# Reordering around the first down columns and the first products of a seven-product feed-forward layer

## What is computed

```python
def swiglu(x, w_gate, w_up, w_down):
    return (jax.nn.silu(x @ w_gate) * (x @ w_up)) @ w_down

h = h + 0.5 * swiglu(rms_norm(h, ffn1_norm[l]), ffn1_w_gate[l], ffn1_w_up[l], ffn1_w_down[l])
...
h = h + 0.5 * swiglu(rms_norm(h, ffn2_norm[l]), ffn2_w_gate[l], ffn2_w_up[l], ffn2_w_down[l])
```

## Time and profile before

| | us |
|---|---|
| median of 3 runs (1808.31 to 1810.58) | 1808.53 |
| the profiled execution | 1809.8 |
| its span, first to last instruction | 1808.0 |
| PE busy (98%) | 1776.7 |
| DVE busy (68%) | 1221.9 |
| ACT busy (47%) | 850.2 |
| POOL busy (15%) | 265.7 |

### The profile page before, as it was taken

The page is one execution under the profiler, slowest core; times in us unless marked ns, Lnnn a source line. Parts: engine busy times, 40 slices in busy tenths (PEclk is TensorE's granted clock), DMA queues, the critical chain, the costliest instruction groups (busy, mean ns, idle before and its releaser), DMA issues.

```text
span 1808.0 us, 24821 instructions
## 1 busy us (share of the span) xinstructions
PE 1776.7 (98%) x9474; PEld 1510.5 (84%) x9474; DVE 1221.9 (68%) x1473; ACT 850.2 (47%) x1197; POOL 265.7 (15%) x270
## 2 busy tenths in 40 slices
PE   9989999999999999989999999999999999999997
PEld 7779989888777788869989988888888888888886
DVE  6577737543677665577746658877577586869884
ACT  5345425433555544335524446454353454466673
POOL 3001101121000002001101140110201102213332
PEclk9999999999999999999999999999999999999999
DMA  6235434244321234324534223232222222233333
GB/s 237 94 102 154 140 113 121 82 144 121 109 86 56 65 102 146 121 94 136 156 107 144 77 87 108 88 100 94 83 92 88 93 88 76 93 98 101 105 128 105
DMA packets 56151, 195.94 MB, mean 108 GB/s; under 512 B 6680, under 2 KB 8856, under 8 KB 56048
## 3 DMA queue, kind: packets, MB, share of 16 engines
q1 hardware_dynamic: 39408, 135.55, 22.9%
q0 software_dynamic: 16208, 58.55, 10.8%
q10 hardware_dynamic: 432, 0.40, 0.1%
HBM read 190.26 MB, written 2.11 MB: 106 GB/s over the span
## 4 chain that ended last, share of the span: by engine, by line
PE 88%; DVE 4%; issue 4%; DMA 2%; ACT 1%; POOL 0%; ACTq 0%; DVEq 0%; POOLq 0%
PE banks L635 23%; PE banks L637 22%; PE banks L636 22%; PE banks L752 4%; PE banks L753 3%; PE banks L754 3%; DMA m<-matrices 2%; DVE w_lo L2054 1%; PE banks L845 1%; PE banks L864 1%; PE banks L888 1%; PE banks L1025 1%; PE banks L1023 1%; PE banks L1024 1%; ACT w_hi L1433 1%
## 5 line engine op out<-in xcount | busy, mean ns | idle before, releaser
L2050 DVE TENSOR_TENSOR w_lo<-w_raw,w_hi 128x1024 fp32r<-128x1024 f32 x249 | 317.1, 1274 | 324.3 <-ACT w_hi L1321 323.2
L1321 ACT ACTIVATE w_hi<-w_raw 128x1024 fp32r<-128x1024 f32 x249 | 263.2, 1057 | 359.3 <-PE banks L637 320.3
L635 PE MATMUL banks<-u_hi,w_hi 128*128 128x512 f32 x1016 | 400.6, 394 | 0.9 <-DVE u_lo L2067 0.9
L637 PE MATMUL banks<-u_hi,w_lo 128*128 128x512 f32 x1016 | 395.8, 390 | 0.0
L636 PE MATMUL banks<-u_lo,w_hi 128*128 128x512 f32 x1016 | 395.4, 389 | 0.0
L635 PEld LDWEIGHTS banks<-u_hi,w_hi 128*128 128x128 f32 x1016 | 190.8, 188 | 42.6 <-issue 2.5
L637 PEld LDWEIGHTS banks<-u_hi,w_lo 128*128 128x128 f32 x1016 | 190.7, 188 | 40.6
L636 PEld LDWEIGHTS banks<-u_lo,w_hi 128*128 128x128 f32 x1016 | 190.9, 188 | 38.7 <-issue 0.5
L2054 DVE TENSOR_TENSOR w_lo<-m,w_hi 128x1024 fp32r<-128x1024 f32 x96 | 116.8, 1222 | 67.4 <-ACT w_hi L1433 67.4
L752 PE MATMUL banks<-xs_hi,w_hi 128*128 128x256 f32 x512 | 147.8, 289 | 12.4 <-DVE w_lo L2054 10.1
L1433 ACT ACTIVATE w_hi<-m 128x1024 fp32r<-128x1024 f32 x96 | 100.2, 1052 | 101.8 <-DMA m<-matrices 46.7
(11 more groups left out here) (383 smaller groups left out, 3384.8 us busy)
## 6 DMA issues: line engine op xcount, KB each, us to landing
w_raw<-weights SPq DMA_DIRECT2D x251, 512.0 KB, 3.5
m<-matrices POOLq DMA_DIRECT2D x64, 512.0 KB, 4.4
mx<-matrices POOLq DMA_DIRECT2D x32, 512.0 KB, 5.4
bias<-neighbour_bias POOLq DMA_DIRECT2D x8, 384.0 KB, 5.1
v_win<-v_a POOLq DMA_DIRECT2D x16, 128.0 KB, 5.2
out_t<-x SPq DMA_DIRECT2D x16, 128.0 KB, 1.8
x<-x_t SPq DMA_DIRECT2D x3, 512.0 KB, 7.1
nm<-gate_rows POOLq DMA_DIRECT2D x4, 256.0 KB, 4.2
```

What stands on the lines that cost most here:

```text
L635: nc.tensor.matmul(o, wh, hi, start=start and k == 0, stop=False)
L637: ins = nc.tensor.matmul(o, wl, hi, start=False, stop=stop and k == len(pairs) - 1)
L1321: nc.scalar.activation(w_hi[:, n.slot, :], w_raw[:, n.slot, :], ACT.Copy).then_inc(hi_ready, 1)
L2050: nc.vector.tensor_tensor(w_lo[:, n.slot, :], w_raw[:, n.slot, :], w_hi[:, n.slot, :].bitcast(F32), ALU.subtract)\
```

## The change

Five edits, all in the feed-forward layer.

- Product order: the first twelve products change places (the copy of kind 1 now has another product between it and kind 6). From product 12 on the list is as before.
- TensorE: the first two of the first 8 down columns are interleaved: the first 5 chunks of column 0, those of column 1, the last chunk of column 0, that of column 1.
- VectorE, plain chunks: `full` stands ahead of chunks 3 and 4 in place of 4 and 5, the four `combo_sum` ahead of chunk 5.
- ScalarE and VectorE beside the first down columns: sums' and quarters' rounded parts and remainders come ahead of the weight splits; VectorE makes the remainders of products 0 and 1 ahead of additions 6 and 7. The steps of pairs 0 and 1 are written out to fit the new product order.
- Second down columns: `mat_low(at + 1)`, the remainder of product 34, stands ahead of the last addition.

```diff
 def sp_products():
-    seq = [(5, 0), (1, 0), (6, 0), (2, 0), (7, 0)]
-    for p in range(N_SP - 1):
+    seq = [(5, 0), (1, 0), (2, 0), (6, 0), (1, 1), (7, 0), (5, 1), (4, 0), (6, 1), (3, 0), (7, 1), (2, 1)]
+    for p in range(1, N_SP - 1):
         seq += [(1, p + 1), (4, p), (5, p + 1), (6, p + 1), (3, p), (7, p + 1), (2, p + 1)]
     return seq + [(4, N_SP - 1), (3, N_SP - 1)]
...
             def down_columns(f, part, u0, g0):
-                chunks = DOWN_PARTS[part]
-                for m in range(DC):
-                    n, g = Lin(u0 + 2 * F_PLAIN + DC * part + m), Lin(g0 + 2 * F_PLAIN + DC * part + m)
-                    unit_ready(n)
-                    bank_free(g)
-                    for k in range(len(chunks)):
+                last = len(DOWN_PARTS[part]) - 1
+                column_at = u0 + 2 * F_PLAIN + DC * part, g0 + 2 * F_PLAIN + DC * part
+
+                def column(m, ks):
+                    n, g = [Lin(at + m) for at in column_at]
+                    if 0 in ks:
+                        unit_ready(n)
+                        bank_free(g)
+                    for k in ks:
...
+                if part == 0:
+                    for ks in (range(last), range(last, last + 1)):
+                        column(0, ks)
+                        column(1, ks)
+                for m in range(2 if part == 0 else 0, DC):
+                    column(m, range(last + 1))
...
                 for m in range(DC - 2):
-                    split_raw(Lin(down[0] + 2 + m))
                     if m < 4:
                         combo_high((T1, T3, T2, T4)[m], m + 1)
-                    else:
-                        quarter_high(m - 4)
-                quarter_high(2)
+                    if m == 4:
+                        quarter_high(0)
+                        quarter_high(1)
+                    if m == 5:
+                        quarter_high(2)
+                    split_raw(Lin(down[0] + 2 + m))
                 for j in range(4):
                     mat_high(j)
                 snap_p1(0)
                 mat_high(4)
-                for p in range(N_SP - 1):
+                mat_high(5)
+                snap_p6(0)
+                mat_high(6)
+                mat_high(7)
+                snap_p7(0)
+                mat_high(8)
+                snap_p1(1)
+                mat_high(9)
+                silu_second(0)
+                mat_high(10)
+                silu_first(0)
+                mat_high(11)
+                for p in range(1, N_SP - 1):
...
-                with dve.Fori(3 if f == 0 else 1, F_PLAIN - 2) as i:
-                    chunk(i, Lin(u0, 2, i), Lin(g0, 2, i))
-                for i in range(F_PLAIN - 2, F_PLAIN):
+                if f > 0:
+                    with dve.Fori(1, F_PLAIN - 3) as i:
+                        chunk(i, Lin(u0, 2, i), Lin(g0, 2, i))
+                for k, i in enumerate(range(F_PLAIN - 3, F_PLAIN)):
                     for m in range(4):
-                        full(4 * (i - F_PLAIN + 2) + m)
+                        if k < 2:
+                            full(4 * k + m)
+                        else:
+                            combo_sum((T1, T3, T2, T4)[m], f)
                     chunk(i, Lin(u0 + 2 * i), Lin(g0 + 2 * i))
...
                 for m in range(DC):
+                    if m < 4:
+                        combo_low((T1, T3, T2, T4)[m], m + 1)
+                    if m == 4:
+                        quarter_low(0)
+                        quarter_low(1)
+                    if m == 5:
+                        quarter_low(2)
                     if m < DC - 2:
                         split_lo(Lin(down[0] + 2 + m))
-                    if m < 4:
-                        combo_sum((T1, T3, T2, T4)[m])
                     else:
-                        combo_low((T1, T3, T2, T4)[m - 4], m - 3)
-                    if m >= 5:
-                        quarter_low(m - 5)
+                        mat_low(m - DC + 2)
                     down_add(0, m)
-                mat_low(0)
-                mat_low(1)
                 first_sums(0)
                 mat_low(2)
                 mat_low(3)
                 last_sum(0)
                 mat_low(4)
-                for p in range(N_SP - 1):
+                mat_low(5)
+                up_first(0)
+                mat_low(6)
+                mat_low(7)
+                first_sums(1)
+                gate_second(0)
+                mat_low(8)
+                mat_low(9)
+                hid_first(0)
+                mat_low(10)
+                mat_low(11)
+                last_sum(1)
+                for p in range(1, N_SP - 1):
...
                             if m < DC - 2:
                                 split_lo(Lin(down[1] + 2 + m))
+                            if m == DC - 1:
+                                mat_low(at + 1)
                             down_add(1, m)
-                    mat_low(at + 1)
-                    if at != DOWN1_AFTER:
-                        if p >= 1:
-                            pair_low(p - 1)
+                    else:
+                        mat_low(at + 1)
+                        pair_low(p - 1)
                         first_sums(p + 1)
```

More of the change, by code:

```diff
@@ L767, in down_columns @@
                             pe.wait_ge(hid_lo_ready, pairs_split(f, 4 * (part - 1) + k // 2))
-                        product(bank[g.slot][:, :], [(k, hid_hi[:, k, :], hid_lo[:, k, :])], n, k == len(chunks) - 1,
-                                start=k == 0, stop=k == len(chunks) - 1)
+                        product(bank[g.slot][:, :], [(k, hid_hi[:, k, :], hid_lo[:, k, :])], n, k == last,
+                                start=k == 0, stop=k == last)
+                if part == 0:
[4 more added lines that the diff above has]
+                    column(m, range(last + 1))
             def ffn(f, q, nu, u0, g0):
@@ L1512, in pairs_high @@
                         snap_p7(p)
-                        if p >= 1:
-                            pair_high(p - 1)
+                        pair_high(p - 1)
                     mat_high(at + 2)
@@ L2157, in ffn, with combo_sum @@
                         u_lo_chunk(nu_next, Lin(e, 2, i), gcol, g_next)
+            def combo_sum(k, f):
+                b11, b12, b21, b22 = [quarter(uf, kh, half) for kh in range(2) for half in (H1, H2)]
+                dve.wait_ge(uf_ready, DC * (f + 1))
+                if k == T2:
+                    dve.wait_ge(xs_sum, 4 * f + 1)
+                if k == T4:
+                    dve.wait_ge(xs_sum, 4 * f + 3)
+                left, right = {T1: (b12, b11), T3: (b22, b12), T2: (b22, combo(xs, T1)), T4: (b21, combo(xs, T2))}[k]
+                nc.vector.tensor_tensor(combo(xs, k), left, right, ALU.subtract).then_inc(xs_sum, 1)
             def pairs_low(f, u0, g0):
@@ L2181, in last_sum @@
                     nc.vector.tensor_tensor(m2[:, :], m2[:, :], m1[:, p % 2, :], ALU.subtract).then_inc(m_summed, 1)
[L2183 to L2191, removed]
                 def combo_low(k, order):
@@ L2260, in pairs_low @@
                 mat_low(4)
-                for p in range(N_SP - 1):
+                mat_low(5)
[11 more added lines that the diff above has]
+                for p in range(1, N_SP - 1):
                     at = SP_AT[1, p + 1]
                     mat_low(at)
-                    if p >= 1:
-                        up_second(p - 1)
-                        hid_second(p - 1)
+                    up_second(p - 1)
+                    hid_second(p - 1)
                     if at == DOWN1_AFTER:
```

## The result

The changed kernel takes 1791.98 us (median of 4 runs, 1791.81 to 1794.09) against 1809.55 for the kernel before on the same chip: ratio 0.9904, 95% interval 0.9892 to 0.9916. The profiled execution took 1791.89 us where the one before took 1809.8; its span fell from 1808.0 to 1790.1 us. The forecast was 1791.4, with a range of 1785.5 to 1796.5. The total is right to 0.6 us; of its terms two were off by about 2 us each, in opposite directions.

The account below looks back on a forecast made before the run. TensorE's matmuls were taken as the bound. Gains of 8.75 + 7.52 + 5.8 = 22.1 us, less 2.0 for the matrix loop and 1.7 for one clock event, gave 18.4: from 1809.8 to 1791.4 us, range 1785.5 to 1796.5.

Parts of the forecast that it names:

- What bounds, and the room: TensorE's matmuls bound the kernel; stretches around both groups of down columns can give back at most 29.5 us together.
- Wait A: At down column 0 of each FFN, TensorE waits 1.16 us for the gate eviction, delayed by the four sums.
- B: At down column 2 of each FFN, a new 2.48 us wait, because interleaved column 1 covers only 0.68 us of the chain.
- Remainders first: In down columns 2 to 7 the waits for x go, and J0 starts at once, where 3.1 us were idle.
- other order: At J2, the new product order needs no snapshot of J1, so 0.8 us per FFN go.
- remainder of product 34: Behind the second down columns, its wait and the clock event go: 3.65 + 2.17 = 5.8 us.
- The matrix loop: Loads on GpSimd's queue delay the snapshot of product 6: 2.0 us more than today, bounds 0.4 and 2.5 per FFN.
- Rival 2: Matrix loop binds in each FFN's first half at its worst period, 8.6 us more: 1800; chance 0.13.
- Rival 3: Matrix loop locks TensorE in the second halves too, 24 us where 3.4 was counted: 1812; chance 0.04.
- Clock: After waits A and B, TensorE's lower clock: one event of 1.7 us taken, bounds 0 and 2.
- Rival 1: At column 2, wait B is hidden, giving 2 x 2.48 us and one event more: 1784.7; chance 0.11.
- Rival 4: hid_lo comes after 82.67, its wait returns ahead of B, up to 1.4 us per FFN: 1794; 0.70 jointly with the forecast.

Follow-up runs that it names:

- kernel 2: Changed kernel with two of the four sums (T2, T4) moved behind the gate eviction of the last plain chunk: 1788.92 us.
- kernel 1: Changed kernel with down columns 0 and 1 run in turn, not interleaved: 1790.52 us.
- kernel 3: Two sums moved as in kernel 2, with only three chunks of column 1 ahead of column 0's last chunk: 1784.75 us.
- kernel 4: On top of kernel 3, column 0's addition put ahead of the subtraction of column 2's weights: 1784.13 us.
- Kernel 7: Kernel before the change with one part alone, the remainder of product 34 ahead of the last addition of the second down columns: 1804.5 us.
- kernel 8: Changed kernel with the old product order and the steps of pairs 0 and 1 as before: 1794.38 us.
- kernel 9: Changed kernel with m3's load ahead of the wait for mx and the accumulating load, from pair 2 on only: 1789.14 us.
- kernel 10: Kernel 4 with the load order of kernel 9: 1780.88 us.
- kernel 5: Changed kernel with m3's load right behind that of mx, ahead of the accumulating load, in every pair with the loop: 1798.64 us.

## Why the prediction was right, point by point

*What bounds, and the room.* Right. All of the gain came from the stretches of the earlier trace rows.

*Wait A.* Right: 1.08 to 1.10 for 1.16, at the place and by the step forecast; kernel 2 takes it away by moving two sums. The bank was used 0.10 us after its eviction, not 0.15, and the sums took 4.73, not 4.75. The 0.08 us for the up eviction shows at the first matmul of column 1. Another 0.08, at the first matmul of column 0 behind A (75.45 to 75.76), was missing in the sum.

*The interleaving moves the wait and does not remove it.* Right, and the most useful step: a wait that no part of the change mentions was found by following who needs column 0's weights and bank. Kernels 1, 3 and 4 show all three of its parts: remove the interleaving and hid_lo comes back, shorten the early part of column 1 and B falls by what was shortened, take the addition off the chain and B falls by its length. The size was 0.16 us low, since I took the end of the last matmul's slot (83.35) for its end, although the step before had been read with the end; and 0.32 us low in the first FFN. What delays ScalarE there is open: the chain calls it issue, and B of the first FFN is 0.31 to 0.35 longer than that of the second in each kernel that has one.

*Remainders first, other order, remainder of product 34.* Right. The waits for x in columns 3 to 7 are gone, J0 follows column 7 at once, 8.63 us for 8.64 from J0 to J3, 5.75 for 5.76 at the two later products. Kernels 7 and 8 show the last two each by itself.

*The matrix loop.* The mechanism was right, the term was wrong: I took 2.0 us more than before, the first profile shows 0.2 less and the second (1.41) the same as before. The second FFN lost nothing in both, below the lower bound of 0.4, and the forecast sign of 1 to 1.7 us in each FFN did not come. The start of the loop came as worked out: m2 of pair 1 was issued at 135.76, 133.9 in the working plus the 1.74 by which J0 was later. What failed is the step behind it. I had added the difference of two periods, 20.89 - 20.16, for each later pair. The three periods of the changed kernel's first half are 20.24, 20.53 and 20.10, so the 20.89 of the earlier trace rows is not a constant. That pass had a slow load of mx, 5.76 us from its issue to that of the accumulation, where the three have 4.78, 4.83 and 4.73; the pass behind it, 20.81 with 4.89, shows that this is not the whole reason. I also wrote that eight down columns let the loop catch up ahead of the second halves. Kernel 7 shows the opposite: the waits came behind J41 and J44 there, 2.1 and 1.5 us in the halves that had none. In the changed kernel, too, 0.95 of the 1.26 us and all of the 1.41 lie in a second half. Over nine profiles of kernels with the loads in their old order, the waits of the loop sum to 1.3 to 4.4 us and lie between none and 2.2 in a half. With m3 earlier from pair 2 on they are zero (kernel 9) and 0.35 (kernel 10). The wait for m3, 0.30 us in the earlier trace rows, went with them, although mx and m3 are then on their way together. So that row showed the place of m3 in the queue, and reading it as a sign of shared DMA engines was wrong. Rivals 2 and 3 rest on the same loop; it never came near their price.

*Clock.* I took one event of two possible, and both came, in both profiles of the changed kernel, and one in kernel 2, which has the same B. Over the six profiles with this B (the changed kernel twice, kernels 2, 5, 8 and 9) an event followed in eleven of twelve cases. So this term was about 1.5 us short; the event in the first FFN cost less than 1.7, since its first 0.5 us fell into the wait. Behind waits of 2.18 and 2.19 us in kernel 1 no event came, behind the 1.25 and 1.60 of kernel 3 none.

*Sum.* The stretches came out 3.9 us worse than the 16.3 forecast (3.2 by two events with the slow first matmuls behind B, 0.64 by B, 0.16 by the slow first matmuls behind A, less 0.15 by A); the sum had 1.7 for one event. That is 2.2 worse, and the loop came out 2.2 better. The two misses cancel, which is luck; the 0.5 us left are those of the u_lo wait. So 1791.4 against 1792.0 is better than the working deserves.

*The other rivals.* Rival 1 (B hidden) is excluded by B itself. Rival 4 (hid_lo after 82.67) did not happen: it was complete at 81.1.

## What to carry to other kernels

When two pieces of work are interleaved to hide a late operand, look at what each of them releases: they now also end together, and with two buffers the next piece finds both busy. Put only as much of the second piece in front as the operand is late, and leave the rest to cover the refill. Where a queue holds loads in order, ask which of them waits for nothing and could stand ahead of a wait, pair by pair, since one pair with another order can spoil the edit.

## What was not expected of the hardware

Issuing m3 beside mx, and not behind its accumulation, took the waits out of the loop, although more is then on its way at once. The time from the issue of mx to that of its accumulation, which waits for mx to land, was 4.73 us in kernel 9 with m3 issued in between (156.31 to 161.04), as in the changed kernel without it (136.28 to 141.06 and 156.52 to 161.35). In kernel 10 it was 5.86 at the same place, but such slow loads come without m3 as well. In the kernel before, in the pass of the earlier trace rows:

```profile
162.71 0.53 POOL L3041 DMA_DIRECT2D mx<-matrices  x1
168.47 0.89 POOL L3059 DMA_DIRECT2D mx<-matrices  x1 [5.24 <-DMA mx<-matrices]
```

From pair 2 on, each of the thirteen profiles has at least one such time of 5.6 to 6.4 us among its twelve, most of the others are 4.7 to 5.0, with m3 beside and without. What makes a load slow is open. Kernel 9 had one of 5.96, in its last pair, and no wait behind it; the changed kernel's 5.88 in the last pair of the first FFN (281.11 to 286.99) was followed by its 0.95 us. The Trainium skill (DMA: Bandwidth & Descriptors, Issuing engines are not separate DMA queues) says that they run on the same 16 DMA engines and interleave; nothing here contradicts that, but the order of issue was the bound, not the sharing.

The same chain of instructions repeats to 0.01 us between executions, whereas the waits of the matrix loop changed place between the two profiles of the changed kernel and by 0.3 and 0.5 us in a half, and the four executions of its second group lie 3.7 us apart. A comparison of kernels that differ by less needs the chain in the trace, not the total.
